# Expert rows gathered as quarter rows and turned on VectorE in 32x32 blocks instead of on TensorE

## The reference, cut to what matters

```python
hn = rms_norm(h, norm_ffn)                 # 544 x 1024
grp, e_idx, w2 = router(hn)                # one group of 8 experts, 2 experts in it
for each expert e:                         # 32 experts
    xe = hn[rows that chose e]             # gathered
    y  = (silu(xe @ w_g[e]) * (xe @ w_u[e])) @ w_d[e]   # 1024->512, 1024->512, 512->1024
    out[rows] += weight * y
h = h + out
```

## Time and profile before

| What | Value |
|---|---|
| time, median of 3 runs | 955.6 us (954.11 to 958.27) |
| profiled execution, first to last instruction (span) | 949.8 us |
| what lies around the span: median less span | 5.8 us |
| TensorE busy with matmuls | 928.6 us (98%) |
| VectorE busy | 547.0 us (58%) |
| DMA queue of SP | 248.51 MB, 67.0% of 16 engines' span |
| DMA queue of GpSimd | 8.93 MB, 2.8% |

### The profile page before, as it was taken

The page is one execution under the profiler, slowest core; times in us unless marked ns, Lnnn a source line. Parts: engine busy times, 40 slices in busy tenths (PEclk is TensorE's granted clock), DMA queues, the critical chain, the costliest instruction groups (busy, mean ns, idle before and its releaser), DMA issues.

```text
span 949.8 us, 11382 instructions
## 1 busy us (share of the span) xinstructions
PE 928.6 (98%) x4433; PEld 469.4 (49%) x4433; DVE 547.0 (58%) x1126; ACT 195.0 (21%) x428; POOL 61.6 (6%) x70
## 2 busy tenths in 40 slices
PE   9999999999999999999999999999999999999997
PEld 5565778876554445634343434334334333334443
DVE  3106442547877311664787787787777575768434
ACT  3111211004746202311111111111111111111401
POOL 3100050000000000010000000000000000000000
PEclk9999999999999999999999999999999999999999
DMA  9690354140004792779999999999999999999211
GB/s 309 203 310 0 102 176 150 53 147 1 1 1 116 234 371 105 294 270 405 419 419 418 419 419 421 419 418 419 420 420 419 419 419 420 419 422 402 99 44 50
DMA packets 74874, 260.57 MB, mean 274 GB/s; under 512 B 12554, under 2 KB 36502, under 8 KB 49956
## 3 DMA queue, kind: packets, MB, share of 16 engines
q1 hardware_dynamic: 69568, 248.51, 67.0%
q0 software_dynamic: 4080, 8.93, 2.8%
q10 hardware_dynamic: 1172, 2.40, 0.6%
HBM read 252.72 MB, written 13.08 MB: 280 GB/s over the span
## 4 chain that ended last, share of the span: by engine, by line
PE 80%; SPq 12%; DMA 4%; DVE 2%; POOL 1%; issue 1%; ACT 0%; DVEq 0%
PE ps L1127 72%; SPq L378 12%; DMA w<-in_w_exp_down 3%; PE ps L1508 2%; PE ps L1778 1%; PE ps L1151 1%; DMA h<-in_x_prompt 1%; DMA mixT<-in_state_conv 1%; PE ps L1813 1%; PE ps L1511 0%; PE ps L1317 0%; PE ps L1248 0%; DVE probs L2344 0%; PE ps L1333 0%; POOL gk L718 0%
## 5 line engine op out<-in xcount | busy, mean ns | idle before, releaser
L1127 PE MATMUL ps<-w,xe 128*64 128x512 f32 x1024 | 229.0, 596 | 9.4 <-DMA w<-in_w_exp_up 8.2
L2718 DVE TENSOR_TENSOR h<-h,ps 128x1024 f32<-128x1024 f32 x120 | 143.2, 1215 | 109.4 <-PE ps L1127 109.3
L1127 PEld LDWEIGHTS ps<-w,xe 128*64 128x64 f32 x1024 | 69.8, 137 | 149.6 <-issue 131.8
L1127 PE MATMUL ps<-w,hT 128*64 128x512 f32 x504 | 115.4, 599 | 0.6 <-DMA w<-in_w_exp_down 0.6
L1127 PE MATMUL ps<-yk,ST 128*128 128x512 f32 (+1 forms) x320 | 105.3, 431 | 0.7 <-DVE yk L2708 0.5
L1127 PE MATMUL ps<-xT,wring 128*128 128x272 f32 x384 | 100.4, 401 | 0.0
L1127 PEld LDWEIGHTS ps<-xT,wring 128*128 128x128 f32 x384 | 68.6, 190 | 24.9 <-issue 12.2
L1127 PE MATMUL ps<-wring,xT 128*32 128x128 f32 (+2 forms) x368 | 77.9, 404 | 0.6 <-DVE xT L2013 0.4
L1127 PEld LDWEIGHTS ps<-yk,ST 128*128 128x128 f32 (+1 forms) x320 | 48.6, 174 | 56.9 <-issue 26.7
L1075 ACT ACTIVATE sg<-ps 64x256 f32<-64x256 f32 x64 | 24.1, 377 | 253.6 <-PE ps L1127 243.0
L758 POOL DMA_INDIRECT xg<-hn_rows,sidx x32 | 32.0, 998 | 645.6 <-PE ps L1778 369.7
(11 more groups left out here) (364 smaller groups left out, 877.8 us busy)
## 6 DMA issues: line engine op xcount, KB each, us to landing
w<-in_w_exp_gate SPq DMA_DIRECT2D x64, 1024.0 KB, 22.4
w<-in_w_exp_up SPq DMA_DIRECT2D x64, 1024.0 KB, 26.3
w<-in_w_exp_down SPq DMA_DIRECT2D x63, 1024.0 KB, 24.3
wring<-in_w_in SPq DMA_DIRECT2D x12, 512.0 KB, 6.5
wpg<-in_w_ple_gate SPq DMA_DIRECT2D x2, 2048.0 KB, 19.3
biaslines<-blrow SPq DMA_DIRECT2D x1, 2560.0 KB, 10.4
h<-in_x_prompt SPq DMA_DIRECT2D x4, 512.0 KB, 9.0
wring<-in_w_in SPq DMA_DIRECT2D x2, 1024.0 KB, 8.1
```

The lines of the kernel that those rows point to most:

```text
L1127: return nc.tensor.matmul(out, l, r, start=start, stop=stop, skip_group_check=skip)
L2718: TTn(h[0:r, t, :], h[0:r, t, :], both(b, r), ALU.add).then_inc(S["hadd"], 1)
```

## The change

Each gathered row now comes in quarters. The indices are `4*row + q` for partition `32q + s` (quarter `q`, slot `s` or `32 + s`), so a table entry has two columns, and `indices` writes them with eight instructions of 32 partitions in place of two of 64. A gather is two indirect DMAs of 128 indices and 1 KB each, for the slots 0 to 31 and 32 to 63. With quarter `q` on the partitions `32q` to `32q+31`, a transpose within blocks of 32x32 on VectorE puts columns of the model dimension on the partitions: partition `32q + i` gets the dimensions `256q + 8i + c`, c = 0 to 7. `rows_T` and its eight-row share of TensorE's order are gone. `x_columns(J)` waits for the gather itself, transposes from `xg` to `xe`, waits for that, and multiplies `xe` in place by `gmix`. `x_tr`, for which the next gather waits, now comes from VectorE. Since partition `p` holds the dimensions `8p` to `8p+7`, `WGU` is laid out anew: piece `k` of gate or up takes the rows `8p + 4k + c`, still 8 KB a partition, now 16 KB apart in memory. `hidden_T(J)` no longer waits for `xT_done` of the next expert; `gate_up(J+1)` waits for it as before. The load of `gex` (one small DMA) goes, and `all_slots` waits for `f_ple`, which says that TensorE has read a tile that it overwrites. The semaphore targets `gathered` and `wout_in` are adapted.

```diff
-        xe = at("xe", [P, 2, 4, P], 72 * K)
+        xe = at("xe", [P, 2, DC, SLOTS], 72 * K)
-        sidx = small("sidx", [P, JOBS], I32)
+        sidx = small("sidx", [P, JOBS, 2], I32)
...
-        WGU = [a[f"w_exp_{x}"].rearrange("e (k p c) n -> e p k (c n)", k=2, c=4) for x in ("gate", "up")]
+        WGU = [a[f"w_exp_{x}"].rearrange("e (p k c) n -> e p k (c n)", k=2, c=4) for x in ("gate", "up")]
...
-                pool.indirect_dma_start(out=xg[:, two(J), :], out_offset=None, in_=hn_d.rearrange("n (k d) -> (n k) d", k=2),
-                                        in_offset=bass.IndirectOffsetOnAxis(ap=at, axis=0), bounds_check=2 * N - 1,
-                                        oob_is_err=False).then_inc(S[f"gath{two(J)}"], 16)
+                for k in range(2):
+                    pool.indirect_dma_start(out=xg[:, two(J), 256 * k:256 * k + 256], out_offset=None,
+                                            in_=hn_d.rearrange("n (q d) -> (n q) d", q=4),
+                                            in_offset=bass.IndirectOffsetOnAxis(ap=at[:, k:k + 1], axis=0), bounds_check=4 * N - 1,
+                                            oob_is_err=False).then_inc(S[f"gath{two(J)}"], 16)
...
-            def rows_T(J):
-                pe.wait_ge(S[f"gath{two(J)}"], gathered(J))
...
-                v = xg[:, two(J), :].rearrange("r (p c) -> r p c", c=4)
-                for c in range(4):
-                    last = T(ps[:, 3, c * P:(c + 1) * P], v[:, :, c], eye(P))
-                last.then_inc(S["x_tr"], 1)
...
-                        last = mm(ps[k * SLOTS:(k + 1) * SLOTS, 0, :], xe[:, b, j, half * SLOTS:(half + 1) * SLOTS],
+                        last = mm(ps[k * SLOTS:(k + 1) * SLOTS, 0, :], xe[:, b, c, :],
...
             def hidden_T(J):
                 pe.wait_ge(S["hm_ok"], J + 1)
...
-                elif J + 1 < NE:
-                    pe.wait_ge(S["xT_done"], J + 2)
+                if isinstance(J, int):
+                    if J:
+                        pe.wait_ge(S["hT_ok"], J)
...
-                if J + 1 < NE:
-                    rows_T(J + 1)
...
-                TS(sidx[0:SLOTS, j0:j0 + n], ps[0:SLOTS, bank, 0:n], 2.0, 2.0 * NOROW, ALU.mult, ALU.add)
-                TS(sidx[SLOTS:P, j0:j0 + n], ps[0:SLOTS, bank, 0:n], 2.0, 2.0 * NOROW + 1.0, ALU.mult, ALU.add).then_inc(S["ix_ok"], 1)
+                for q in range(4):
+                    for k in range(2):
+                        last = TS(sidx[32 * q:32 * q + 32, j0:j0 + n, k], ps[32 * k:32 * k + 32, bank, 0:n], 4.0, 4.0 * NOROW + q, ALU.mult, ALU.add)
+                last.then_inc(S["ix_ok"], 1)
...
+                dve.wait_ge(S["f_ple"], 6)
...
             def x_columns(J):
 
                 b = two(J)
-                dve.wait_ge(S["x_tr"], J + 1)
+                dve.wait_ge(S[f"gath{b}"], gathered(J))
...
-                TTn(xe[:, b, :, :].rearrange("p c (k s) -> p c k s", k=2), ps[:, 3, :].rearrange("p (c k s) -> p c k s", k=2, s=SLOTS),
-                    gex[:].rearrange("p k c -> p c k").unsqueeze(3).broadcast_to([P, 4, 2, SLOTS]), ALU.mult).then_inc(S["xT_done"], 1)
+                V.transpose(xe[:, b, :, :].rearrange("p c (k s) -> p c k s", k=2),
+                            xg[:, b, :].rearrange("p (k s c) -> p c k s", k=2, c=DC)).then_inc(S["x_tr"], 1)
+                dve.wait_ge(S["x_tr"], J + 1)
+                TTn(xe[:, b, :, :], xe[:, b, :, :], gmix[:].unsqueeze(2).broadcast_to([P, DC, SLOTS]), ALU.mult)\
+                    .then_inc(S["xT_done"], 1)
```

More of the change, by code:

```diff
@@ L270, in build @@
         gple = small("gple", [P, DC])
-        gex = small("gex", [P, 2, 4])
         gq = small("gq", [P, 1])
@@ L319, in build @@
         pgi = small("pgi", [P, NPG + 1], I32)
-        sidx = small("sidx", [P, JOBS], I32)
-        icur = small("icur", [P, 1], I32)
+        sidx = small("sidx", [P, JOBS, 2], I32)
+        icur = small("icur", [P, 2], I32)
         plTs = small("plTs", [P, 2, NS])
@@ L764, in _ @@
                     pool.wait_ge(S["x_tr"], J - 1)
-                gather(J, sidx[:, J:J + 1])
+                gather(J, sidx[:, J, :])
             nov = overflow_jobs(pool)
@@ L775, in gather_job @@
                 pool.sem_inc(S["passed"], 1)
-                gather(J, icur[:, 0:1])
+                gather(J, icur[:, :])
             overflow(pool, nov, gather_job)
@@ L1762, in _ @@
             project(3, 0)
-            def rows_T(J):
-                pe.wait_ge(S[f"gath{two(J)}"], gathered(J))
-                if not isinstance(J, int):
-                    pe.wait_ge(S["hT_ok"], J)
-                    pe.sem_inc(S["passed"], 1)
-                elif J >= 2:
-                    pe.wait_ge(S["hT_ok"], J - 1)
-                elif J:
-                    pe.wait_ge(S["xT_done"], J)
-                else:
-                    pe.wait_ge(S["f_pl"], 6)
-                v = xg[:, two(J), :].rearrange("r (p c) -> r p c", c=4)
-                for c in range(4):
-                    last = T(ps[:, 3, c * P:(c + 1) * P], v[:, :, c], eye(P))
-                last.then_inc(S["x_tr"], 1)
             def gate_up(J, part):
@@ L1802, in hidden_T @@
                 pe.wait_ge(S["hm_ok"], J + 1)
[L1803 to L1806 removed]
+                if isinstance(J, int):
+                    if J:
+                        pe.wait_ge(S["hT_ok"], J)
+                    else:
+                        pe.wait_ge(S["f_pl"], 6)
                 else:
                     pe.wait_ge(S["hT_ok"], J)
[L1809 removed]
                     pe.sem_inc(S["passed"], 1)
```

14 lines of the change are left out of this document (4 added, 10 removed).

## The result

| | median us | runs | ratio to before | 95% interval |
|---|---|---|---|---|
| before | 957.74 | 12 | | |
| changed kernel | 962.44 | 12 | 1.0052 | 1.0035 to 1.0068 |

The change costs 5.0 us (3.4 to 6.5) by the ratio, 4.7 by the medians. The forecast was 958.8, which is +3.2 on before's first three runs (955.6), with 953 to 966 as its range and "no change within 0.5%" as the likeliest case. Over 12 runs before's median is 957.74, 2.1 higher. So of the 3.6 us between 958.8 and 962.44, 2.1 are the base and 1.5 the change. The time lies in the range. It is above the 960.4 from which the forecast counted as slower; the ratio lies at that edge (0.5%).

The account below looks back on a forecast made before the run. The prediction took one stream of weights to set the loop's end. +1.9 us (start) and +1.3 (stream) gave +3.2 on a span of 949.8, 953.0; with 5.8 around it, 958.8 us, range 953 to 966.

Parts of the forecast that it names:

- What bounds the kernel: Expert loop: one weight stream at 419 GB/s sets the end, some 15.3 us an expert; a delayed start passes on one for one.
- The start: Index writing to first gate and up matmuls: +1.9 us, from some +0.3 to +3.5.
- The indices: VectorE before the first gather: eight index instructions for two, 0.19 us each, +1.1 us.
- The second gather: POOL, ahead of expert 0: two indirect DMAs for one, +1.3 us, bounds 0 and 2.7.
- The turn: Ahead of expert 0: VectorE transpose and multiply take 1.47 us for TensorE's 1.96, -0.5 us.
- The stream: Loop's DMA: gathered rows in 1 KB instead of 2 KB pieces slow it by +1.3 us, bounds 0 and +2.6.
- The steps of 16 KB: Gate and up weight loads: 8 KB runs at 16 KB steps taken to cost 0, bounded at +21 us.
- Does TensorE stay ahead: Loop: an expert takes TensorE some 13.85 us for 14.01, leaving 14 us of slack at the loop's end.
- the transpose was slow: Rival, VectorE's x_columns: a transpose above 1.2 us makes TensorE wait; 962 us at twice, 997 at four times; 6 in 100.
- weights at steps: Rival, every gate and up piece: 16 KB steps slow the stream, up to +21 us, 980, middle 969; 6 in 100.
- TensorE as the bound of a faster loop: Rival, expert loop: TensorE bounds it after all, so it gets faster, 941 to 955.6 us; 8 in 100.
- the hidden start: Rival, ahead of expert 0: half gathers overlap, indices and small pieces cost nothing, 955 to 957 us; part of the forecast's range.

Follow-up runs that it names:

- addition first: Changed kernel with VectorE's addition of combine unit 1 of expert J-2 moved ahead of the transpose and multiply of expert J+1: 962.38 us, 1.0047.
- 2 KB pieces: Changed kernel with before's single gather per expert and two index instructions, output differs: 960.64 us, 1.0026; with plsq's transfer also issued first, 958.82 us, 1.0011.
- filler: Changed kernel with 14 unread transposes on TensorE in its idle gap before expert 0: 961.43 us, 1.0053; also one of four edits made together: 959.59 us, 1.0041.
- second trace of before: Kernel before, unchanged, run and profiled again: ratio 1.0012.
- late indices: Kernel before with 24 more index-kind instructions on VectorE ahead of the index instructions, results unread: 964.04 us, 1.0062.

## Why the prediction was right

**What bounds the kernel: right for before, at the edge for the changed kernel.** In before it is the stream, from load 3 to the last weights: delaying the start by 5.2 us cost 5.9. The landing at 865.84, read there as the last weights, is of expert 30's `down`; expert 31's is issued behind it. In the changed kernel TensorE and the stream meet: it waits for weights by only 0.3 us, taking 0.3 us an expert from TensorE (addition first) gained nothing, and with 2 KB pieces it no longer waits for them at all.

**The start: the sum was too large, its parts differ.** Expected +1.9, and 1.5 to 2.5 us later; `gate_up(0)` is 1.15 us later behind the first index instruction (8.32 or 8.33 for 7.17 in all four traces with the changed kernel's gathers and no filler; 7.21 in the second trace of before). The indices cost what was said (1.57 us for 0.37, and the gather leaves 1.19 later). The second gather was mis-sized: +1.3 taken, +0.05 in this pair of traces, near its lower bound of 0. From the first gather's issue to the turn it is 3.9 to 4.6 us in eight traces with two gathers of 1 KB pieces released together and 3.1 to 4.4 in five with one of 2 KB, so in single traces the second costs between nothing and some 0.7. The turn gave 0.1 for 0.5, since the transpose is 1.09 to 1.16 us. Together 0.75 too much. The Trainium skill, "Vector Engine (DVE) Microarchitecture Reference", section 3.8, has the 32x32 transpose at one element per cycle per lane; here the transpose of 128x512 in fp32 takes 1.11 us and the multiply of the same shape 0.69, so the estimate that it is as cheap does not hold for this instruction. It reads `xg` at steps of 8 elements; whether the transpose or this reading costs the 0.42 us was not tried.

**Not seen: TensorE's clock at the start.** I counted the four transposes as time removed and not as what kept a gap short. Where the clock falls load 3 goes out 1.6 to 1.7 us later.

**The stream: direction right, size small.** Without the hole, load 3 to the last group is 518.4 to 519.2 us in four traces with 1 KB pieces and 516.3 to 517.9 in four with 2 KB: means 518.7 and 516.8, +1.9 us for +1.3 taken, inside its bounds of 0 and 2.6. By the fixed overhead in the Trainium skill, "DMA: Bandwidth & Descriptors", section "Why small descriptors are slow (HBM only)", the prediction had an estimate of 0.5; the measurement is above both, with twice as many DMAs beside the smaller pieces. The steps of 16 KB cost nothing, as taken. Another part lies outside the span: 2.3 us for 1.85 with two gathers an expert. I had no term for it.

**Does TensorE stay ahead: right by little.** The transpose was to bind from 1.2 us, and it is 1.11. The mechanism is the one foretold (unit 4 waits for addition 1), and the wrong term is the price of the transpose, 1.11 us for 0.69: with the expert at 14.33 us for 13.85 the slack went from 8.2 us of waits to 0.3 and not up to 14. The text's own sign of a wrong step, "an expert at 14.3 us or more with no waits for weights", came true. That it was still free is shown by the addition moved ahead.

**Not seen: the hole.** In one place, expert 2, ScalarE's silu waits for a small transfer. In before it waits too, but VectorE is then busy with an addition, and its multiply starts right behind that:

```profile
447.67 0.77 ACT L1075 ACTIVATE sg<-ps 64x256 f32<-64x256 f32 x2 [10.21 <-DMA embed_rows_sample<-plsq]
447.77 1.22 DVE L2718 TENSOR_TENSOR h<-h,ps 128x1024 f32<-128x1024 f32 x1 [4.39 <-PE ps L1127]
449.02 0.98 DVE L2682 SCALAR_TENSOR_TENSOR sg<-sg,wsl,ps 64x256 f32<-64x256 f32 x2
```

There silu starts 0.1 us ahead of the addition, in the changed kernel 2.1 us behind the start of it (456.99 and 454.85). TensorE, without its transposes, comes to the addition 0.7 us sooner behind `gate_up(0)` (34.3 us for 35.0), and from the issue of the small transfer to silu it is 13.0 us for 11.3; why it takes longer is open. The later start is not the cause: with late indices the start is 5.2 us later and there is no hole. VectorE's dearer transpose comes on top, and TensorE stands 2.24 us. It costs 1.3 us by the bytes, 1.6 by the means with and without it (520.3 and 518.7, 1 KB pieces), 1.6 with a standard error of 0.5 by the times with 2 KB pieces.

**The sum.** 1.15 (start) + 0 to 1.7 (clock) + 1.9 (pieces) + 1.6 (hole) + 0.45 (outside the span) = 5.1 to 6.8, measured 5.0 (3.4 to 6.5). The 0.5 us of the last expert are in no term of their own: they lie between the same two points as the pieces and the hole. So the forecast of +3.2 came out as near as it did in part by luck. It had 0.75 us too much at the start and lacked 2.65 to 4.35: 0.6 of the pieces, the hole, what lies outside the span, and the clock. The rivals: the transpose was slow, but below the price at which it decides; weights at steps are out; TensorE as the bound of a faster loop is out, since the expert did not get shorter; the hidden start is out, by the late indices.

## What to carry to other kernels

An instruction taken from the engine that seems busiest may have been what kept a gap short: count the gaps that are left, and what the clock does behind them, before the microseconds removed. Where an engine and a stream just meet, a small delay is free (0.32 us an expert) and the next one is not, and it can cost more than itself (1.1 us of work became 2.7 an expert). And look for the one iteration in which something else is waited for: a loop's average hides it.
